# Where on-chip tensors begin within 512 bytes, in a two-block fp32 transformer kernel that is bound by its matmuls

## What is computed

```python
# first block
x = x + 0.5 * rms_norm(swiglu_ffn(rms_norm(x, norm_pre[l, 0]), ffn1_w_in[l], ffn1_w_out[l]), norm_post[l, 0])
mixed = token_mixer(rms_norm(x, norm_pre[l, 1]), w_mix_in[l], ...)      # HGRN2 heads and mLSTM heads
x = x + rms_norm(mixed, norm_post[l, 1])
x = x + 0.5 * rms_norm(swiglu_ffn(rms_norm(x, norm_pre[l, 2]), ffn2_w_in[l], ffn2_w_out[l]), norm_post[l, 2])
# second block, twice
x = layer_norm(alpha * x + mix, ...)                                     # mixer_ab, then mixer_c
x = layer_norm(alpha * x + cross_attend(x, mem, wq, wkv, wo), ...)       # 256 memory rows, 4 heads
x = layer_norm(alpha * x + conv_ffn(x, w_up, conv_w, conv_b, w_down), ...)
```

## Time and profile before

| what | value |
|---|---|
| median of three runs | 2442.83 us (2442.2 to 2443.79) |
| the profiled execution's own time | 2443.0 us |
| its span, first to last instruction | 2441.2 us |
| TensorE matmuls busy | 2403.7 us, 98% |
| TensorE weight loads busy | 2036.4 us, 83% |
| VectorE, ScalarE, GpSimd busy | 1099.8, 810.3, 65.6 us |
| mean granted TensorE clock | 0.992 of full speed |

### The profile page before, as it was taken

How to read it: one execution, slowest core, us unless ns; L and a number is a source line. 1 busy time by engine, 2 the same in 40 slices (tenths; PEclk the granted TensorE clock), 3 DMA queues, 4 the chain that set the end, 5 groups by cost and what they waited for, 6 DMA issues and landing times.

```text
span 2441.2 us, 27031 instructions
## 1 busy us (share of the span) xinstructions
PE 2403.7 (98%) x12164; PEld 2036.4 (83%) x12164; DVE 1099.8 (45%) x1036; ACT 810.3 (33%) x888; POOL 65.6 (3%) x39
## 2 busy tenths in 40 slices
PE   9999999999889999999999999999999999999998
PEld 8888889897678888898987888888888977888887
DVE  4333226574453333147635644423544636544424
ACT  4222225454342222133332333322322342433311
POOL 0000000220100000000001000000000000000000
PEclk9999999999899999999999999999999999999999
DMA  4222223212022222232430322232332511222321
GB/s 161 93 97 104 104 86 130 70 36 85 18 104 87 104 95 104 104 143 70 157 120 26 113 104 87 103 118 72 123 119 87 190 69 69 87 103 88 118 92 66
DMA packets 34405, 238.30 MB, mean 98 GB/s; under 512 B 3949, under 2 KB 4333, under 8 KB 6514
## 3 DMA queue, kind: packets, MB, share of 16 engines
q1 hardware_dynamic: 34288, 236.56, 27.0%
q10 hardware_dynamic: 2, 0.00, 0.0%
HBM read 234.46 MB, written 2.10 MB: 97 GB/s over the span
## 4 chain that ended last, share of the span: by engine, by line
PE 96%; DVE 2%; ACT 2%; issue 0%; DMA 0%; ACTq 0%; DVEq 0%
PE bank L435 53%; PE bank L509 28%; PE bank L839 4%; PE bank L474 3%; PE bank L497 1%; PE bank L866 1%; PE bank L692 1%; PE bank L886 1%; PE bank L627 1%; ACT w_hi L1009 0%; DVE w_lo L1452 0%; DVE xn L1477 0%; PE bank L596 0%; ACT junk L1029 0%; PE bank L877 0%
## 5 line engine op out<-in xcount | busy, mean ns | idle before, releaser
L435 PE MATMUL bank<-a_hi,w_hi 128*128 128x512 f32 (+1 forms) x2112 | 787.4, 373 | 0.6 <-DVE a_lo L1501 0.6
L435 PE MATMUL bank<-a_lo,w_hi 128*128 128x512 f32 (+1 forms) x2112 | 782.4, 370 | 0.0
L435 PE MATMUL bank<-a_hi,w_lo 128*128 128x512 f32 (+1 forms) x2112 | 782.4, 370 | 0.0
L1452 DVE TENSOR_TENSOR w_lo<-raw,w_hi 128x2048 fp32r<-128x2048 f32 x207 | 477.1, 2305 | 525.7 <-ACT w_hi L1009 525.0
L1009 ACT ACTIVATE w_hi<-raw 128x2048 fp32r<-128x2048 f32 x207 | 394.6, 1907 | 365.2 <-DMA raw<-w_full 365.2
L435 PEld LDWEIGHTS bank<-a_hi,w_hi 128*128 128x128 f32 x2112 | 399.1, 189 | 71.0 <-issue 2.3
L435 PEld LDWEIGHTS bank<-a_lo,w_hi 128*128 128x128 f32 x2112 | 398.8, 189 | 68.1
L435 PEld LDWEIGHTS bank<-a_hi,w_lo 128*128 128x128 f32 x2112 | 399.2, 189 | 67.4 <-issue 0.7
L509 PE MATMUL bank<-w_hi,h_hi 128*128 128x512 f32 x704 | 274.4, 390 | 0.0
L509 PE MATMUL bank<-w_hi,h_lo 128*128 128x512 f32 x704 | 273.9, 389 | 0.0
L509 PE MATMUL bank<-w_lo,h_hi 128*128 128x512 f32 x704 | 273.9, 389 | 0.0
(11 more groups left out here) (274 smaller groups left out, 2331.7 us busy)
## 6 DMA issues: line engine op xcount, KB each, us to landing
raw<-w_full SPq DMA_DIRECT2D x207, 1024.0 KB, 4.8
rows_ab<-rows SPq DMA_DIRECT2D x8, 1024.0 KB, 5.2
x<-x SPq DMA_DIRECT2D x4, 512.0 KB, 6.0
mem_raw<-mem SPq DMA_DIRECT2D x2, 1024.0 KB, 8.1
out<-x SPq DMA_DIRECT2D x4, 512.0 KB, 2.6
raw<-w_full SPq DMA_DIRECT2D x2, 512.0 KB, 6.4
ab_rows<-ab_rows SPq DMA_DIRECT2D x1, 768.0 KB, 7.7
wg_raw<-w_gates SPq DMA_DIRECT2D x1, 512.0 KB, 5.6
```

What stands on the lines that cost most here:

```text
L435: last = mm(bank[:, b + m, cols], w[:, s, c0:c0 + P], act_in[:, k, cols], start=(k == 0 and j == 0), stop=(k == KD - 1 and j == 2))
L1452: V.tensor_tensor(w_lo[:, u % SLOTS, :], raw[:, u % SLOTS, :], w_hi[:, u % SLOTS, :], ALU.subtract).then_inc(w_split, 1)
```

## The change

Some tensors begin elsewhere within 512 bytes. Sizes, slices, instructions and their order stay.

```diff
-        a_hi = at("a_hi", [P, KD, T], f32r, X0 + 16 * KB)
-        a_lo = at("a_lo", [P, KD, T], f32r, X0 + 32 * KB)
-
-        raw = at("raw", [P, SLOTS, FULL], f32, X0 + 48 * KB)
-        w_lo = at("w_lo", [P, SLOTS, FULL], f32r, X0 + 48 * KB)
-        w_hi = at("w_hi", [P, SLOTS, FULL], f32r, X0 + 80 * KB)
-        C0 = X0 + 112 * KB
+
+        a_hi = at("a_hi", [P, KD, T], f32r, X0 + 16 * KB + 128)
+        a_lo = at("a_lo", [P, KD, T], f32r, X0 + 32 * KB + 128)
+        W0 = X0 + 48 * KB + 320
+
+        raw = at("raw", [P, SLOTS, FULL], f32, W0)
+        w_lo = at("w_lo", [P, SLOTS, FULL], f32r, W0)
+        w_hi = at("w_hi", [P, SLOTS, FULL], f32r, W0 + 32 * KB)
+        C0 = W0 + 64 * KB
...
-        mem_hi = arena("mem_hi", [P, KD, MEM], f32r, 64)
-        mem_lo = arena("mem_lo", [P, KD, MEM], f32r, 72)
-        k_mem = arena("k_mem", [P, KD, MEM], f32, 80)
+        mem_hi = arena("mem_hi", [P, KD, MEM], f32r, 64.125)
+        mem_lo = arena("mem_lo", [P, KD, MEM], f32r, 72.125)
+        k_mem = arena("k_mem", [P, KD, MEM], f32, 80.125)
...
-        o_hi = arena("o_hi", [P, KD, T], f32r, 48)
-        o_lo = arena("o_lo", [P, KD, T], f32r, 64)
+        o_hi = arena("o_hi", [P, KD, T], f32r, 47.875)
+        o_lo = arena("o_lo", [P, KD, T], f32r, 63.875)
```

More of the change, by code:

```diff
@@ L86, in build @@
         stat = at("stat", [P, NT, 8], f32, C1 + 32)
-        row0 = at("row0", [1, D], f32, X0 + 80 * KB)
+        row0 = at("row0", [1, D], f32, W0 + 32 * KB)
         bnl = at("bnl", [P, NT, 12], f32, C1 + 160)
@@ L99, in build @@
         conv_out = arena("conv_out", [P, 2, T], f32, 96)
-        rows_ab = arena("rows_ab", [P, 2, D], f32, 88.0625)
-        ln_u = arena("ln_u", [P, 2, D], f32, 96.0625)
+        rows_ab = arena("rows_ab", [P, 2, D], f32, 88.125)
+        ln_u = arena("ln_u", [P, 2, D], f32, 96.125)
         res = arena("res", [P, 2, D], f32, 0)
@@ L133, in build @@
         row_em = arena("row_em", [HEADS, T], f32, 94.0625)
[L134 to L139, removed]
+        masks = arena("masks", [P, 8, P], u32, 96.125)
+        gbias = arena("gbias", [P, 2], f32, 100.125)
+        ct = arena("ct", [P, 2, NT, HEADS], f32, 100.1875)
+        mcol = arena("mcol", [P, 4, NT], f32, 100.3125)
+        hcol = arena("hcol", [P, NT, HEADS], f32, 100.375)
+        g_end = arena("g_end", [P, HEADS * NT], f32, 100.4375)
         mtmp = arena("mtmp", [P, T], f32, 100.5)
```

## The result

The changed kernel takes **2453.19 us** (median of 5 runs, 2452.59 to 2455.71) against 2442.99 us before in the same comparison. The ratio is 1.0041, 95% interval 1.0026 to 1.0055: **0.4% slower, by 10.2 us**, clear of what a measurement of this kernel can tell from no change. The prediction was 2337 us, 4.3% faster, and the result lies outside its range.

A forecast was written before the change was run, and what follows sets the result against it. TensorE was taken as the bound, its f32r matmuls paying 13.3 ns each beyond streaming. Savings of 100.2 and 10.7 us less 5 us given back made 105.9 us, so 2443 became 2337 us; range 2320 to 2446 us.

The forecast's parts named there:

- Terms 3 and 4: f32 matmuls and transposes, and the splits on VectorE and ScalarE with 64-byte moves: no effect on time, 0 each.
- the rival of a fixed price: f32r matmuls: the 13.3 ns stay whatever the addresses, all terms 0, no change at 2443 us; chance 0.25.
- Term 1: f32r pairs at distance 192, lines 435, 509, 839: remainder 13.3 falls to 2.2 ns, 9024 matmuls save 100.2 us.
- Term 2: f32r pairs at 320 or 64, lines 474, 509, 839: half the relief on 1920 matmuls, saving 10.7 us.
- Term 5: Where TensorE waits for vector work, mainly the mixer's end: faster matmuls wait sooner, 5 us given back.
- the likeliest case: All f32r pairs: relief as summed, 2337 us, with its own range 2320 to 2370 us; chance 0.42.
- The slower rival: Up and down, lines 435 and 509: streams stay at 231.1 ns instead of 226.7, 2480 to 2495 us; chance 0.15.
- A pace that differs between lines 435 and 509 (437 and 511 now), though both are at 192,: Sign of wrong: weights stationary and `h` stationary differ in pace at 192, so distance alone is not what counts.

The follow-up runs named there:

- map: Small kernel without the model, streaming f32r matmuls at distances 0 to 496 bytes in steps of 16; 512 columns took 226.7 ns at 0, 228.9 at 192.
- map2: Second small kernel without the model, varying load length, operand type and the f32 matmuls ahead; at 512 columns bf16 took 215.8 ns, f32 429.2.
- five maps: Small kernels without the model, timing matmul streams over distances, load lengths, types, entries and common shifts; lowest f32r pace at 512 columns 226.7 ns.
- w64: Layout of before with the weights alone moved by 64 bytes; 2480.44 us in a single run.
- w320: Layout of before with the weights alone moved by 320 bytes; 2483.19 us, ratio 1.0151.
- same128: Layout of before with every f32r operand of the products 128 bytes further on, distances 0 again except the gates' 24 matmuls; 2444.4 us, ratio 0.9997.

## Why the prediction was wrong, point by point

**The bound and the pace** were right: TensorE is busy 98% of the span before and 99% after, lines 435, 509, 839 and 474 are 88% of the chain and their successors as much, and their matmuls follow each other at 226.7 and 120.0 ns before. Outside the first mixer the pieces of f32r matmuls named above are together 11.5 us longer by their pace. With the measured paces in place of the assumed remainder, the prediction's own sum comes out (an estimate, with 228.9 ns for the 7488 of 512 columns at 192, 233.3 for the 768 at 320 and 64, 117.8 and 113.4 for the 1536 and 1152 of 256 columns): 7488 x 2.2 + 768 x 6.6 - 1536 x 2.2 - 1152 x 6.6 ns = +10.6 us, against +10.2 measured. Terms 3 and 4 were right: the f32 pieces are the same to the hundredth of a microsecond, and the splits take 2.31 and 1.91 us as before.

**That the 13.3 ns are not a fixed price** was right, and so was the reading of the earlier trace rows: what moves after an f32 matmul is a stream that falls into a repeating phase. Such phases are in the map: spacings of 231 and 236 ns in turn at distance 64, 229, 232 and 226 at 192, an even 226 to 227 at 0. That an address costs nothing, as it would by the rival of a fixed price, is not borne out for f32r: with nothing but addresses changed the pace went from 226.7 to 233.4 ns in the map, and to 239.2 with both operands off by 4 bytes. bf16 and f32 kept their pace at each distance tried. Whether it is the two reads that meet, as the prediction pictured it, no run shows: from 459.46 to 464 us of before, at the slow matmuls and at the steady ones alike, the load starts within 0.01 us of the matmul.

**Term 1 failed**, and with it the sign. Its price was 2.2 ns at distance 192, taken from the f32 rows as the case "with the conflict absent". No run shows 2.2 ns: f32 has 429.2 ns on map2, 2.5 over twice 213.3, and f32r at 192 has 228.9, a remainder of 15.6. What failed is the step from f32 to f32r: no distance, entry or length of load in five maps brought 512 columns of f32r under 13.3 ns. The floor of another operand type was no lower bound that could be reached, let alone the value to take. "0, where both reads begin in the same place, is the least likely to be the best" was argued from a picture and is the reverse of the map: nothing in it is better than 0. With 7488 matmuls at 192 the term came out at +16.5 us for 512 columns (7488 x 2.2 ns) where the prediction had -83 (7488 x 11.1).

**Term 2**, half the relief at 320 and 64, failed for 512 columns (233.4 ns, +6.6 instead of -5.6) and had the right sign for 256: 6.6 ns less, where 11.1 was the full price. The prediction treated both widths as one, on the ground that both pay 13.3 ns at distance 0. Away from 0 they part: 192 costs 512 columns 2.2 ns and gives 256 columns 2.2.

**Term 5**, what waits take back, was priced for a faster kernel and was not put to the test.

**The range.** 2370 us as the upper end of the likeliest case does not follow from its own words: two thirds of term 1 are 66.8 us, which leaves 2376 us or more. The chances and the whole range do not hang on it.

**The slower rival** was what happened, by its own test: the pace in up1 is above 226.7 ns. It put 231.1 ns on 9024 pairs and +40 to +48 us. Measured: 228.9 on the 7488 of 512 columns at 192, 233.3 on 768 others, and 256 columns faster, for +10.2, a quarter of its low end. The result lies between the range (up to 2446 us) and this rival (from 2480), where the prediction had nothing. Its phase was one that streams pass through; the one they stay in at 192 repeats three spacings near 226, 229 and 232 ns, mean 228.9. It had 0.15, and the range left it out.

**A pace that differs between lines 435 and 509 (437 and 511 now), though both are at 192,** was named as a sign that distance is not all. The two lines did not differ there, at 228.9 both. But two paces at one distance were in the changed kernel's own trace, line 476 at 113.5 and 117.8 ns, and then in the experiments, as down0 against down2 and as 76 against 76.

What stays open: what the 13.3 ns themselves are. They do not shrink with the length of the load (32 columns leave 18.3 at distance 0), they are not made by other engines (map has 226.7 ns with the others idle), and bf16 and f32 have 2.5 ns in their place (215.8 and 429.2 ns at 512 columns). Every f32r matmul of every run has a load beside it, so that the load causes them at all is not shown; a stream that keeps one stationary operand without loading it again would have told. What selects the phase in the whole kernel, why an entry that differs by a nanosecond ends in another one, and why 16 bytes and 32 bytes differ, was not found.

## What to carry to other kernels

A remainder on each instruction of the bound engine is worth a map: one small kernel with a block for each address, width and type, on a line of its own, gave more than any argument from the trace, and it should come before a layout is moved, not after. Take no floor from another operand type. A map's block is one sample of an entry: vary the entry, and keep the class of places in which the map was made, before carrying it into the full kernel.

## What the runs showed of the hardware that was not expected

- The pace of an f32r stream depends on where its two operands begin relative to each other, in the first map with a period of 256 bytes: 226.7 to 234.4 ns at 512 columns and 113.3 to 120.1 at 256 in steps of 16 bytes. bf16 (215.8 ns) and f32 (429.2 ns) did not depend on it at the distances tried.
- The same form at the same distance runs at 228.9 ns in one network and at 233.3 in another (107.14 and 109.20 us for 468), in w64 and in w320 alike. In map2 one block at 192 runs at 233.3 behind 3 f32 matmuls and at 228.9 behind 1, 2 and 5 to 8; that what runs ahead selects the pace, there or here, is the author's reading and not shown.
- Both operands 4 bytes on cost 12.5 ns a matmul, 239.2 against 226.7; both 16 bytes on 6.6; both 32 bytes on nothing.
- In the mixer the granted clock falls to 0.50 of full speed for short spells that differ between executions (34 us of them before, 31 in the changed kernel); the stretch took 325.6 to 334.4 us in the profiled executions (of kernels with somewhat different paces), and the runs of one kernel scatter by as much (2440.5 to 2448.9 us in same128).
